# A Conformer convolution in a three-layer block: two of four channel tiles convolved on TensorE instead of one

## The reference

```python
def depthwise_conv(x, w):
    pad = (w.shape[0] - 1) // 2
    return lax.conv_general_dilated(x, w[:, None, :].astype(x.dtype), (1,), [(pad, pad)],
                                    dimension_numbers=('NWC', 'WIO', 'NWC'),
                                    feature_group_count=x.shape[-1])

def conformer_conv(u, dw_w, dw_b, ln_g, ln_b):
    a, gate = jnp.split(u, 2, -1)
    h = a * jax.nn.sigmoid(gate)
    h = depthwise_conv(h, dw_w) + dw_b
    return jax.nn.silu(layer_norm(h, ln_g, ln_b))

# in even_mixer, for the tokens and again for the context:
    q, k, v = mla_qkv(u[..., :MLA_IN], *mla_p, rope_cs=rope_cs)
    o_conv = conformer_conv(u[..., MLA_IN:], dw_w, dw_b, ln_g, ln_b)
```

## The kernel before

| Steps k | What `latent_inputs` puts ahead of them |
|---|---|
| 0 to 5 | norms of the query and key latents: squares on ScalarE (L465), sums on VectorE (L468), square root on ScalarE (L472), reciprocal and products on VectorE (L475, L482) |
| 6 | transposes of the query latent (L2401), copied out by ScalarE (L2406) |
| 8 | query products (L380 with `cqT`), copied out by ScalarE |
| 16 | transposes of the key latent (L2401), copied out by ScalarE |
| 17 | key and value products (L380 with `ckvT`), copied out by ScalarE |
| 23 to 25 | head norm of the queries (L465, L468, L472, L475, L482, L485) |
| 26, 27 | rotary turn of the queries on VectorE (L2219 to L2225), then their transposes (L403) |
| 28 to 30 | keys gathered on VectorE (L2453, L2455), head norm of the keys |
| after the last tap | end of the keys' head norm; then `convolved` (L2166), the last call of `on_tensor`, and VectorE and TensorE both wait for `diag_out`, the copy out of the convolved tile |

## Time and profile before

### The profile page before, as it was taken

One profiled execution on the slowest core, in us unless ns is written; L12 is line 12 of the kernel. 1 busy time (PEld: TensorE's weight loads), 2 busy tenths in 40 slices (PEclk: granted clock), 3 DMA queues, 4 the chain that ended last, 5 costly groups with the idle time before them and its releaser, 6 DMA issues. The chain is left out here.

```text
span 4357.6 us, 51328 instructions
## 1 busy us (share of the span) xinstructions
PE 3532.0 (81%) x21676; PEld 2057.9 (47%) x21676; DVE 1206.0 (28%) x2334; ACT 639.3 (15%) x1235; POOL 324.0 (7%) x463
## 2 busy tenths in 40 slices
PE   7998778898897787669749999789876899757776
PEld 3767437556552354347633333255765636422222
DVE  2212230231332115856230000033444335220000
ACT  1103100111101101333110000022221013100000
POOL 0000000000000000000011111103434100000000
PEclk9997889998898898889869999899777799889999
DMA  3110122243444210000339999730100301289999
GB/s 125 58 39 1 39 92 84 88 146 97 133 144 181 65 39 13 10 30 1 143 108 401 394 396 397 271 117 25 22 17 16 107 29 66 102 301 401 404 403 359
DMA packets 263832, 638.53 MB, mean 147 GB/s; under 512 B 63780, under 2 KB 114676, under 8 KB 256310
## 3 DMA queue, kind: packets, MB, share of 16 engines
q1 hardware_dynamic: 253558, 612.19, 37.7%
q0 software_dynamic: 10048, 23.07, 2.3%
HBM read 594.18 MB, written 41.04 MB: 146 GB/s over the span
## 5 line engine op out<-in xcount | busy, mean ns | idle before, releaser
L380 PE MATMUL bank<-weights_l,hT_l 128*128 128x256 f32 (+3 forms) x1552 | 485.0, 475 | 23.8 <-DMA weights_l<-in_w_in 19.4
L380 PEld LDWEIGHTS bank<-weights_l,hT_l 128*128 128x128 f32 (+1 forms) x1552 | 337.1, 221 | 169.2 <-issue 102.7
L376 PE MATMUL bank<-hT_l,weights_l 128*128 128x512 f32 (+1 forms) x928 | 331.9, 520 | 29.0 <-DMA weights_l<-in_w_in 23.7
L1729 PE MATMUL bank<-expert_weights_l,expert_tokensT_l 128*32 128x512 f32 x3072 | 337.5, 595 | 11.8 <-DMA expert_weights_l<-in_moe_w 10.0
L1934 PE MATMUL bank<-expert_weights_l,expert_tokensT_l 128*64 128x512 f32 x1024 | 239.8, 615 | 80.2 <-DMA expert_weights_l<-in_moe_w 79.1
L376 PEld LDWEIGHTS bank<-hT_l,weights_l 128*128 128x128 f32 x928 | 179.3, 194 | 179.5 <-issue 155.4
L1242 PE MATMUL bank<-hT_l,gate_weights_r 128*128 128x512 f32 x384 | 211.7, 703 | 21.3 <-DMA gate_weights_r<-in_w_in 21.3
L1729 PEld LDWEIGHTS bank<-expert_weights_l,expert_tokensT_l 128*32 128x32 f32 x3072 | 108.5, 110 | 227.1 <-issue 220.7
L1612 POOL DMA_INDIRECT expert_rows_l<-normed_rows,row_numbers_l x16 | 15.4, 963 | 2674.2 <-DVE row_numbers_l L1608 2669.9
L1934 PEld LDWEIGHTS bank<-expert_weights_l,expert_tokensT_l 128*64 128x64 f32 x1024 | 79.1, 140 | 230.5 <-issue 175.6
L1764 PE MATMUL bank<-expert_weights_l,rows 128*32 128x512 f32 x1536 | 167.9, 592 | 0.9 <-ACT rows L1804 0.9
(11 more groups left out here) (494 smaller groups left out, 4808.1 us busy)
## 6 DMA issues: line engine op xcount, KB each, us to landing
expert_weights_l<-in_moe_w SPq DMA_DIRECT2D x192, 2048.0 KB, 25.1
ada_weights_r<-in_ada_w SPq DMA_DIRECT2D x48, 1024.0 KB, 4.9
weights_l<-in_w_in SPq DMA_DIRECT2D x10, 2048.0 KB, 7.6
weights_l<-in_w_in SPq DMA_DIRECT2D x16, 1024.0 KB, 5.4
gate_weights_r<-in_w_in SPq DMA_DIRECT2D x12, 1024.0 KB, 6.2
weights_l<-in_od_w_in SPq DMA_DIRECT2D x7, 1024.0 KB, 5.7
gate<-gate_rows_r SPq DMA_DIRECT2D x24, 256.0 KB, 2.5
weights_l<-in_ev_w_in SPq DMA_DIRECT2D x3, 2048.0 KB, 10.2
```

The lines of the kernel that those rows point to most:

```text
L376: ins = pe.matmul(bank[:n, :m], w_sb[:, k, s:s + n], xT[:, k, t:t + m], start=k == 0, stop=k == kt - 1)
L380: ins = pe.matmul(bank[:rows_of_tile(x), :n], x, w_sb[:, k, :n], start=k == 0, stop=k == kt - 1)
L1729: return pe.matmul(bank[q * STRIP:(q + 1) * STRIP, :], xs[:, k, e, g * STRIP:(g + 1) * STRIP], w[:, j, h * HALF:(h + 1) * HALF], start=k = ...
```

## The change

`TILES_ON_TENSOR` goes from 1 to 2. VectorE keeps tiles 2 and 3, so a tap is four instructions instead of six. TensorE gets tiles 0 and 1, 16 blocks of diagonals instead of 8, and each call site now puts two blocks in the queue: tile 0 at `k` = 3 to 15, tile 1 at `k` = 19 to 27 and after the last tap. The two PSUM banks and the ring of two blocks are shared by the two tiles, one after the other. Lines after L2163 stand one or two lower in the changed file.

```diff
 CONV_CT = CONV_CH // P
-TILES_ON_TENSOR = 1
+TILES_ON_TENSOR = 2
 CONV_PAD = (CONV_K - 1) // 2
...
             dve.wait_ge(link.sem, link.n)
             if k % 4 == 3:
-                on_tensor(*blocks.pop(0))
+                for _ in range(TILES_ON_TENSOR):
+                    on_tensor(*blocks.pop(0))
             yield True
         convolved = Signal(nc, "channels_convolved")
         dve.tensor_copy(taps[:, CT - 1, 0:1], taps[:, CT - 1, 0:1]).then_inc(convolved.sem, convolved.one())
-        on_tensor(*blocks.pop(0))
+        while blocks:
+            on_tensor(*blocks.pop(0))
         for eng in (pe, dve):
             eng.wait_ge(diag_out.sem, diag_out.n)
```

## The result

The change takes 4368.67 us (median of 7 runs, 4365.70 to 4371.65) against 4356.08 us before (7 runs, 4348.12 to 4361.89). The ratio is 1.0034, with a 95% interval of 1.0022 to 1.0045: it is slower, by 12.6 us by the medians, which is 0.3%. The profiled execution took 4370.2 us, its span is 4368.5 us.

The account below looks back on a forecast made before the run. TensorE's queue was taken to bound the middle, from query transposes to key and value products, and VectorE the ends. Terms summed to +13.3 us, 4372.7 for the profiled execution, 4370.6 from the median; range 4363 to 4378.

Parts of the forecast that it names:

- k = 3: Ahead of the query latent's transposes: two blocks delay them though VectorE's taps shorten, +0.9 us, bounds −1.3 to +3.2.
- k = 7: Between the transposes and the query products: a second block at full clock adds 5.3 us, bounds +3.5 to +7.1.
- k = 11 and 15: Behind the query products, before the key and value products: two blocks become four, back to back, +10.6 us.
- k = 16: Tile 0's copy out stands ahead of ScalarE's key latent copies, delaying key and value products: +0.5 us, bounds 0 to +1.1.
- k = 19 to 24: Forecast at k = 19 to 25: extra diagonals +1.2 us, shorter tap −1.1, four blocks hidden in TensorE's pause; net +0.1.
- taps 25, 28 to 30: Late taps in VectorE's own chain, k = 25, 28, 29 and 30, become shorter: −4.4 us.
- the end: VectorE waits for tile 1's copy out before the keys' rotary turn: 0 to 1.3 us, taken as +0.3.
- The clock's rival: TensorE, more evenly occupied, loses both clock drops, at the transposes and k = 7: +8.4 us, 4365.7; chance 14%.
- VectorE as the chain: Added blocks fit TensorE's pauses and nine shorter VectorE taps come through: −9.8 us, 4347.5; chance 7%.
- ScalarE's queue: Slow blocks at k = 19 and 23 delay diagonals and the root behind them: about +20 us, 4377; chance 10%.
- nothing to measure: For another cause, the shifts sum by chance inside a spread like the three runs' 7.7 us; chance 5%.
- The signs: Shorter tap rows, 248 L2137 records, VectorE idle over 50 us, key and value products about 17 us later, attention at about 1921.

Follow-up runs that it names:

- the halves: Against the kernel before: tile 0 convolved twice on TensorE, VectorE's three tiles kept, ratio 1.0044; separately, VectorE's taps 1 to 30 of tile 1 left out, 0.9982.
- the moved blocks: Kernel before, TensorE's blocks of k = 7, 11 and 15 moved behind the key and value products: 4338.12 us, ratio 0.9953; repeated on another chip, 0.9967.
- the first two runs: Kernel before with only TensorE's added work, stage 239.02 us, and with only VectorE's taps 1 to 30 of tile 1 left out, stage 210.97 us.
- the fuller shared tile: TensorE convolves tile 0 and 24 taps of tile 1, blocks placed where it waits, against the kernel before: 4331.33 us, ratio 0.9946, stage 189.76 us.
- three orders: Tiles 0 and 1 on TensorE: the change's order, 231.95 us; more blocks late, 219.95; blocks at the start and behind the key and value products, 200.20.
- four splits in one kind of placement: TensorE blocks kept out of the middle: tile 0 alone, 207.23 us; tiles 0 and 1, 200.20; tile 0 with 20 taps of tile 1, 186.85; with 24, 183.66.
- the mended version: Tile 0 and 24 taps of tile 1 on TensorE, block 10's diagonals and products moved earlier, against the kernel before: 4321.90 us, ratio 0.9933.
- the shared-tile kernel: TensorE convolves tile 0 and 20 taps of tile 1, blocks placed where it waits, against the kernel before: ratio 0.9942; repeated, 4328.49 us, 0.9935.

## Why the prediction was right, step by step

The forecast was slower by 13.3 us to 4370.6; the median is 4368.67, 12.6 above before. That is closer than the sum deserves, since the stage that the sum is about grew by 10.70. The mechanism is the one forecast: the halves run alone, and the moved blocks, show it by experiment. The terms, with each measured shift taken between the rows of before and after that bound its place (1.15 us added for the earlier start):

| Place | Predicted | Measured | From |
|---|---|---|---|
| k = 3 | +0.9 | +0.92 | transposes 1716.72 to 1716.49 |
| the transposes and the wait behind them | not in the sum | −0.86 | 3.85 to 2.34 us, wait 1.88 to 2.53 |
| k = 7 | +5.3 | +5.16 | 7.12 to 12.28 us |
| k = 11 and 15 | +10.6 | +9.03 | 10.59 to 19.62 us |
| k = 16 | +0.5 | +0.43 | wait 1.60 to 2.02 |
| k = 19 to 24 | +0.1 | +0.11 | reciprocal 1802.97 to 1816.61 |
| taps 25, 28 to 30 | −4.4 | −4.35 | to `convolved`, 1862.20 to 1871.49 |
| the end | +0.3 | +0.26 | from `convolved` to the attention, 45.38 to 45.64 us |
| sum | +13.3 | +10.70 | |

**What was mis-sized.** "Two blocks become four, back to back": +10.6. A tile has 31 taps, so its eighth block has three, and tile 0's now stands at k = 15. The row has 60 records, not 64. Fifteen taps for eight is seven taps at 1.32 us, 9.3. I had counted the seven taps at the end and not here. The order of instructions shown with the change had it (15 diagonals in that row).

**Agreement by chance at k = 3.** TensorE's first block started 18.17 us into the stage, 1.35 earlier than before and not 1.09, and from there to the transposes it took 13.14 us and not 12.87. The two misses, of 0.3 each, cancel.

**What was missing.** The transposes of the query latent had a granted clock of 1.00, where it was 0.56 before; TensorE came to them from two blocks and not from a pause of 3.31 us. I had named this in a rival and not priced it. ScalarE's copies then set the next start, so only 0.86 of 1.51 us came through.

**The wait at the end** was forecast at 0 to 1.3 us and was 0: the copy out ended at 1870.88, 0.6 before VectorE came. The 0.26 us in that line of the table is something else: VectorE pauses for 0.43 us within the first of the keys' rotary turns (L2221), where it did not before, and the trace names no other engine for it. The agreement with +0.3 is chance.

**The rivals.** The clock's rival was right for the transposes alone. At k = 7 the clock fell as before, and the two blocks took 12.28 us where two at full clock take 10.59. These are the granted clocks (us, PE busy, PEclk, DMA share, GB/s), first in the transposes before, then in the first block at k = 7 after the change:

```profile
1718.00:1720.00 2.00, 2.00 (x12) 0.50 0.88 299
1724.00:1726.00 2.00, 2.00 (x5) 0.51 0.00 0
```

The rule that it named, of the Trainium skill (TensorE: Matmul & The Clock Gate, What's actually happening), fits the transposes in both directions: at full clock (1.00) behind blocks, partly at half (0.56 on average) behind a pause.

VectorE as the chain fell with the first two runs. The argument against it counted five added blocks ahead of the last key and value product; they are four (k = 3, 7, 11 and 15), 21.2 us of work for 8.4 us of pauses, and it holds with four. ScalarE's queue did not become the chain in the change, by 0.4 us; it did in the fuller shared tile, at the keys' root, through the same mechanism. That there would be nothing to measure fell with the ratio.

**The signs.** VectorE's idle time before the queries' sums, forecast at over 50 us, was 55.83; its 120 instructions of L2157 took 66.1 us (forecast some 65), and L2137 has 248 records. No block took over 7 us in the middle of the stretch (15 taps in 19.62). Later places came early by what the sum had too much: counted from the start of the stage, the key and value products 14.7 us later and not 17, the attention's first product 10.7 and not 13.3.

## What to carry to other kernels

When two engines share a job, ask for each stretch which of them the rest of the chain is waiting for; on this evidence a transfer of work is a gain only where the receiving engine pauses and the giving one does not. Where the order is written out by hand, the place of a piece is worth at least as much as the split: two tiles on TensorE gave 232, 220 and 200 us for the stage in three orders, and the old split with three blocks moved gave 204 in place of 221, while four splits in one kind of placement lie between 184 and 207. After each move look for what is queued behind a new wait, on the engine that only helps (here ScalarE's diagonals ahead of a square root): one late set of diagonals cost 6 us through three engines.

## What the runs showed of the hardware that I had not expected

TensorE's short pauses cost more than their length when transposes follow. The queries' 48 transpose records took 7.68 to 8.42 us behind pauses of 4.8 to 24 us in eight traces, at a mean granted clock of 0.65 to 0.73, and 6.02 to 6.07 us at 1.00 in the four in which a block of products ran up to within 1.5 us of them. In the thirteenth trace, of the mended version, they came right behind a block too, at 1.00, in two rows of 1.47 and 4.62 us with a wait of 0.54 between. A whole row of query products, otherwise 23.38 to 23.46 us, took 25.16 in the second trace of the shared-tile kernel, behind a wait of 2.76 us where the other kernels of that placement had 2.25 to 2.59. The granted clock in that row was 0.93, against 1.00 in the first trace of the same kernel, so such a row is not fixed even for one kernel.
